# A two-direction scan by head pairs: scores and turned factors from one product each, with an identity stored beside keys and queries

## The reference

```
def step(s, inp):
    r_t, w_t, k_t, v_t, a_t, b_t = inp
    sa = einsum('bhvk,bhk->bhv', s, a_t)
    s = s * w_t + sa * b_t + v_t * k_t          # outer products over v and k
    return s, einsum('bhvk,bhk->bhv', s, r_t)
```

## Time and profile before

| | us |
|---|---|
| three runs | 4171.22 (median), 4166.51, 4188.89 |
| the profiled execution, its own time | 4177.35 |
| its span in the profile | 4175.7 |
| busy in the span: PE / PEld | 3887.3 (93%) / 2497.7 (60%) |
| busy: DVE / ACT / POOL | 1563.2 / 852.1 / 772.0 |
| mean granted clock of TensorE | 0.986 of full speed |

### The profile page before, as it was taken

How to read it: one execution, slowest core, us unless ns; L and a number is a source line. 1 busy time by engine, 2 the same in 40 slices (tenths; PEclk the granted TensorE clock), 3 DMA queues, 4 the chain that set the end, 5 groups by cost and what they waited for, 6 DMA issues and landing times.

```text
span 4175.7 us, 93934 instructions
## 1 busy us (share of the span) xinstructions
PE 3887.3 (93%) x40168; PEld 2497.7 (60%) x40168; DVE 1563.2 (37%) x3295; ACT 852.1 (20%) x1872; POOL 772.0 (18%) x634
## 2 busy tenths in 40 slices
PE   5999999989988888888999999999999999999998
PEld 4544444455467767777444434457688854658887
DVE  1411111154644444444222212444344424525363
ACT  2200000020145545445100001115000011420000
POOL 3100000000133333333000000000334310013343
PEclk8999999999999999999999999999999999999999
DMA  8289999942200000000379996110122221102221
GB/s 347 116 321 355 361 353 358 372 183 74 84 8 16 13 12 12 12 12 13 141 333 428 429 428 280 61 61 1 69 93 81 83 87 41 41 21 81 97 85 41
DMA packets 56386, 627.10 MB, mean 150 GB/s; under 512 B 5904, under 2 KB 9232, under 8 KB 20496
## 3 DMA queue, kind: packets, MB, share of 16 engines
q1 hardware_dynamic: 49664, 599.41, 36.2%
q0 software_dynamic: 3968, 14.16, 1.2%
q10 hardware_dynamic: 2448, 9.05, 0.6%
HBM read 604.50 MB, written 18.09 MB: 149 GB/s over the span
## 4 chain that ended last, share of the span: by engine, by line
PE 83%; issue 5%; DVE 5%; DMA 4%; ACT 1%; DVEq 1%; PEld 0%; SPq 0%; ACTq 0%; PEldq 0%
PE bank L919 63%; PE bank L1401 13%; DMA ring<-slabs 2%; DMA work<-slabs 2%; PE bank L1808 1%; PE bank L947 1%; PE bank L1816 1%; PE bank L1825 1%; PE bank L1452 1%; DVE hx L2539 0%; PE bank L1814 0%; DVE work L2848 0%; PE bank L1811 0%; DVE resc L2760 0%; DVE work L2717 0%
## 5 line engine op out<-in xcount | busy, mean ns | idle before, releaser
L919 PE MATMUL bank<-ring,work 128*32 128x256 f32 (+3 forms) x7002 | 763.2, 438 | 67.4 <-DMA ring<-slabs 58.8
L919 PE MATMUL bank<-work 128*128 128x256 f32 (+7 forms) x3478 | 713.3, 416 | 13.4 <-DVE work L3233 4.8
L919 PEld LDWEIGHTS bank<-work 128*128 128x128 f32 (+3 forms) x3478 | 463.3, 178 | 247.3 <-issue 185.5
L919 PEld LDWEIGHTS bank<-ring,work 128*32 128x32 f32 (+2 forms) x7002 | 316.7, 124 | 488.6 <-issue 382.5
L919 PE MATMUL bank<-hx,ring 128*128 128x512 f32 (+1 forms) x1344 | 484.3, 514 | 4.9 <-DVE hx L2539 2.8
L919 PE MATMUL bank<-work,ring 128*128 128x256 f32 (+1 forms) x1616 | 478.6, 454 | 9.2 <-DVE work L2804 5.5
L919 PEld LDWEIGHTS bank<-work,ring 128*128 128x128 f32 x1616 | 305.3, 190 | 176.1 <-issue 130.8
L1401 PE MATMUL bank<-work 64*64 64x64 f32 x11520 | 327.1, 227 | 67.9 <-issue 54.1
L919 PEld LDWEIGHTS bank<-hx,ring 128*128 128x128 f32 x1344 | 253.5, 190 | 223.6 <-issue 201.6
L3431 POOL TENSOR_TENSOR work<-ring 128x512 f32<-128x512 f32 (+1 forms) x44 | 69.3, 1575 | 1622.1 <-ACT work L2037 1224.4
L1401 PEld LDWEIGHTS bank<-work 64*64 64x64 f32 x11520 | 293.7, 139 | 94.9 <-issue 92.4
(11 more groups left out here) (336 smaller groups left out, 4830.4 us busy)
## 6 DMA issues: line engine op xcount, KB each, us to landing
ring<-slabs SPq DMA_DIRECT2D x228, 2048.0 KB, 9.7
work<-slabs SPq DMA_DIRECT2D x48, 2048.0 KB, 18.3
work<-kv SPq DMA_DIRECT2D x18, 384.0 KB, 3.1
kv<-work SPq DMA_DIRECT2D x2, 3072.0 KB, 15.7
kv<-work ACTq DMA_DIRECT2D x6, 512.0 KB, 18.1
work<-tabs ACTq DMA_DIRECT2D x1, 2176.0 KB, 8.3
resx<-xT SPq DMA_DIRECT2D x1, 2048.0 KB, 11.2
kv<-work POOLq DMA_DIRECT2D x1, 2048.0 KB, 7.1
```

Source lines behind the costliest of these rows:

```text
L919: return pe.matmul(out, lhsT, rhs, start=(k == 0), stop=(k == n - 1))
```

## The change

- Scores and two of the three transposes come from one product. An identity is stored between the factors of each two chunks: `ar` becomes `arc` (batch 0, for two chunks: key, identity, key) and `arx` (batches 1 and 2: key, queries, identity, key, queries). An even chunk takes key, queries, identity; an odd one identity, key, queries: 192 contiguous columns, or 128 in batch 0. `bd` against these gives its scores and its transpose, `kd` the same. The transpose of `ar`'s key stays a product of its own, now within `scores`. `turned_keys` and the steps ba and kt of TensorE are gone.
- sb now fills two banks (4 and 5) and sk two (0 and 1) for every batch, in place of one each. ACT takes all of sb: NT, QB, and two copies of 256 columns (key to BK, `ar`'s to AM). DVE takes all of sk, with a copy of 256 columns, kt, that ACT had.
- `chunk_products` takes BK and QB of a chunk in one product of 128 columns, whose moving operand is two blocks of 64 columns far apart in one tile (`BKQ`); the kv terms stand behind it.
- The order of TensorE, ACT and DVE is changed as the diff shows; wu 1 moves ahead of scores 1, and nothing stands between mean and W 0.
- `decayed_sums` is four instructions on DVE in place of one; `decayed_queries` writes with another stride; four copies write the identities once, during the mixing.

```diff
-    RK_PE += [("sb", _a, 0), ("sk", _a, 0), ("wu", _d, 0), ("ba", _a, 0), ("kt", _a, 0), ("sb", _a, 1), ("sk", _a, 1)]
-    RK_PE += [("wu", _d, 1), ("wu", _d, 2)] + ([] if _d else [("mean",)]) + [("ba", _a, 1), ("kt", _a, 1)]
+    RK_PE += [("sb", _a, 0), ("sk", _a, 0), ("wu", _d, 0), ("wu", _d, 1), ("sb", _a, 1), ("sk", _a, 1), ("wu", _d, 2)] + ([] if _d else [("mean",)])
     RK_PE += [("ar", _d, 0), ("kv", _d, 0), ("sb", _a, 2), ("sk", _a, 2), ("bc", _d, 0), ("ar", _d, 1), ("kv", _d, 1)]
-    RK_PE += [("ba", _a, 2), ("kt", _a, 2), ("bc", _d, 1), ("y", _d, 1), ("kv", _d, 2), ("ar", _d, 2), ("bc", _d, 2), ("y", _d, 2)]
+    RK_PE += [("bc", _d, 1), ("y", _d, 1), ("kv", _d, 2), ("ar", _d, 2), ("bc", _d, 2), ("y", _d, 2)]
...
-    RK_DVE += [("res",), ("bonus",)] * _d + [("mt", _a, 0)]
-    RK_DVE += [("mt", _a, 1)] + ([] if _d else [("cen",)]) + [("ar", _d, 0), ("mt", _a, 2), ("bc", _d, 0)]
+    RK_DVE += [("res",), ("bonus",)] * _d + [("mt", _a, 0), ("kt", _a, 0)]
+    RK_DVE += [("mt", _a, 1), ("kt", _a, 1)] + ([] if _d else [("cen",)]) + [("ar", _d, 0), ("mt", _a, 2), ("kt", _a, 2), ("bc", _d, 0)]
...
-    RK_ACT += [("nt", _a, 0), ("wu", _d, 0), ("ba", _a, 0), ("kt", _a, 0), ("nt", _a, 1), ("wu", _d, 1), ("wu", _d, 2)]
-    RK_ACT += [("ba", _a, 1), ("kt", _a, 1)] + ([] if _d else [("sq",)]) + [("nt", _a, 2), ("ba", _a, 2), ("kt", _a, 2)]
+    RK_ACT += [("nt", _a, 0), ("ba", _a, 0), ("wu", _d, 0), ("wu", _d, 1), ("nt", _a, 1), ("ba", _a, 1), ("wu", _d, 2)]
+    RK_ACT += ([] if _d else [("sq",)]) + [("nt", _a, 2), ("ba", _a, 2)]
...
+    elif _k == "sb":
+        RK_READ[_name] = {_b: [("act", ("nt",) + _rest), ("act", ("ba",) + _rest)] for _b in (4, 5)}
+    elif _k == "sk":
+        RK_READ[_name] = {_b: [("dve", ("kt",) + _rest)] for _b in (0, 1)}
...
-        ar = [cut(ring_b, at, NCH, 2 * CH) for at in (0, 1536)]
-        E3 = ring_b[:, 3072:3840]
-        BA = [z[:, 0:2 * NCH * 2 * CH].rearrange("p (h c n) -> p h c n", h=2, c=NCH)[:, :, :, 0:CH] for z in (hxf, ring_a)]
+            blocks = z[:, 0:o].rearrange("p (m n) -> p m n", n=CH)
+            BKQ.append([blocks[:, 2 * c:2 * NCH * 2 + c - GC + 1:2 * NCH * 2 - c - GC, :] for c in range(GC, NCH)])
+        arc = [cut(ring_b, at, GC // 2, 3, CH) for at in (0, 1664)]
+        arx = [cut(ring_b, at, NCX // 2, 5, CH) for at in (384, 2048)]
+        E3 = ring_b[:, 3328:4096]
...
-                n = 2 * CH if b else CH
-                outb, = banks(p, "sb", d, b, after=[("pool", 0, "arr", d), ("dve", 0, "ara", d)])
-                outk, = banks(p, "sk", d, b)
+                banks(p, "sb", d, b, after=[("pool", 0, "arr", d), ("dve", 0, "ara", d)])
+                banks(p, "sk", d, b)
+                outb, outk = score_banks("sb"), score_banks("sk")
                 for q, c in enumerate(chunks(b)):
-                    mb = heads2(outb[:, q * 128:q * 128 + n], bd[:, c * CH:(c + 1) * CH], ar[d][:, c, 0:n])
-                    mk = heads2(outk[:, q * 128:q * 128 + n], kd[:, c * CH:(c + 1) * CH], ar[d][:, c, 0:n], across=True)
+                    odd, at = c % 2, 256 * q - 64 * (c % 2)
+                    if b:
+                        factors = arx[d][:, c // 2 - GC // 2, 2 * odd:2 * odd + 3, :]
+                        a = arx[d][:, c // 2 - GC // 2, 3 * odd, :]
+                    else:
+                        factors, a = arc[d][:, c // 2, odd:odd + 2, :], arc[d][:, c // 2, 2 * odd, :]
+
+                    def places(out):
+
+                        if b:
+                            return out[:, at:at + 192].rearrange("p (m n) -> p m n", m=3)
+                        if odd:
+                            return out[:, at:at + 128].rearrange("p (m n) -> p m n", m=2)
+                        return out[:, at:at + 256].rearrange("p (m n) -> p m n", m=2)[:, :, 0:CH]
+
+                    heads2(places(outb), bd[:, c * CH:(c + 1) * CH], factors)
+                    turned = 512 * (q // 2) + 384 + 64 * odd
+                    mb = turn2(outb[:, turned:turned + CH], a)
+                    mk = heads2(places(outk), kd[:, c * CH:(c + 1) * CH], factors, across=True)
                 mb.then_inc(rk_pe, rk.next("sb", d, b))
                 mk.then_inc(rk_pe, rk.one("sk", d, b))
-
-            def turned_keys(p, d, b):
-
-                outb, = banks(p, "ba", d, b)
-                outk, = banks(p, "kt", d, b)
-                for q, c in enumerate(chunks(b)):
-                    turn2(outb[:, q * CH:(q + 1) * CH], bd[:, c * CH:(c + 1) * CH])
-                    mb = turn2(outb[:, 256 + q * CH:256 + (q + 1) * CH], ar[d][:, c, 0:CH])
-                    mk = turn2(outk[:, q * CH:(q + 1) * CH], kd[:, c * CH:(c + 1) * CH], across=True)
-                mb.then_inc(rk_pe, rk.next("ba", d, b))
-                mk.then_inc(rk_pe, rk.one("kt", d, b))
...
-                    m = heads2(out[:, q * 128:q * 128 + CH], WU[:, c, 0:CH], BK[d][:, c, 0:CH])
+                    if b:
+                        m = heads2(out[:, q * 128:(q + 1) * 128].rearrange("p (m n) -> p m n", m=2), WU[:, c, 0:CH], BKQ[d][c - GC])
+                    else:
+                        m = heads2(out[:, q * 128:q * 128 + CH], WU[:, c, 0:CH], BK[d][:, c, 0:CH])
                     if beside is not None:
-                        mo = other_term(others, d, beside, q, 0)
-                    if b:
-                        m = heads2(out[:, q * 128 + CH:(q + 1) * 128], WU[:, c, 0:CH], QB[d][:, c - GC, :])
-                        if beside is not None:
-                            mo = other_term(others, d, beside, q, 1)
+                        for part in range(2 if b else 1):
+                            mo = other_term(others, d, beside, q, part)
...
                     scores(p, a, 0)
                     inverse_times(p, d, 0)
-                    turned_keys(p, a, 0)
+                    inverse_times(p, d, 1)
                     scores(p, a, 1)
-                    inverse_times(p, d, 1)
                     inverse_times(p, d, 2)
                     if d == 0:
                         head_sums(p, "mean", Y, "dve", ("yf", 1))
-                    turned_keys(p, a, 1)
                     chunk_products(p, d, 0, beside=0)
                     scores(p, a, 2)
                     chunk_sums(p, d, 0)
                     chunk_products(p, d, 1, beside=1)
-                    turned_keys(p, a, 2)
...
+            def factors_turned(p, d, b):
+
+                cs_ = slice(GC * b, GC * b + GC)
+                act.wait_ge(*rk_done("pe", p, "sb", d, b))
+                act.activation(BK[d][:, cs_, 0:CH].rearrange(PAIRED, i=2), factor_copies("sb", "key"), ACT.Copy)
+                copied(p, AM[d][:, cs_, 0:CH].rearrange(PAIRED, i=2), factor_copies("sb", "a"), "ba", d, b)
...
+                keys = kn.rearrange(CHUNKED, c=NCH)
+                for out, c, last in ((arc[d][:, :, 0, :], 0, GC), (arc[d][:, :, 2, :], 1, GC), (arx[d][:, :, 0, :], GC, NCH), (arx[d][:, :, 3, :], GC + 1, NCH)):
+                    m = v.scalar_tensor_tensor(out, keys[:, c:last:2, :], -1.0, lw65[:, c:last:2, 1:65], ALU.mult, ALU.mult)
+                m.then_inc(rk_dve, rk.next("ara", d))
+
+            def identities():
+
+                for d in range(2):
+                    v.tensor_copy(arc[d][:, :, 1, :], bc(eye2.unsqueeze(1), 128, GC // 2, CH))
+                    v.tensor_copy(arx[d][:, :, 2, :], bc(eye2.unsqueeze(1), 128, NCX // 2, CH))
...
+                v.tensor_copy(BK[d][:, cs_, CH:128].rearrange(PAIRED, i=2), factor_copies("sk", "key")).then_inc(rk_dve, rk.one("kt", d, b))
```

More of the change, by code:

```diff
@@ L164 @@
         RK_READ[_name] = {}
+    elif _k == "sb":
+        RK_READ[_name] = {_b: [("act", ("nt",) + _rest), ("act", ("ba",) + _rest)] for _b in (4, 5)}
+    elif _k == "sk":
+        RK_READ[_name] = {_b: [("dve", ("kt",) + _rest)] for _b in (0, 1)}
     else:
-        _by = {"sb": ("act", ("nt",) + _rest), "sk": ("dve", ("mt",) + _rest), "mean": ("dve", ("cen",)), "gate": ("dve", ("res",))}
+        _by = {"mean": ("dve", ("cen",)), "gate": ("dve", ("res",))}
         _by.update({_q: ("dve", _name) for _q in ("x0", "ar", "bonus")}, T=("lvd", _name))
@@ L617, in build @@
         ring_a, ring_b = (flat(ring[(E0 + q) % RING]) for q in (6, 5))
-        BK, AM, QB, QK = [], [], [], []
+        BK, AM, QB, QK, BKQ = [], [], [], [], []
         for z in (hxf, ring_a):
@@ L797, in rk_bank, with score_banks, factor_copies @@
             return P[list(RK_READ[name])[0]]
+        def score_banks(name):
+            b = {"sb": 4, "sk": 0}[name]
+            return PB[:, b:b + 2, :].rearrange("p x n -> p (x n)")
+        def factor_copies(name, kind):
+            b, at = {"sb": 4, "sk": 0}[name], {"key": 128, "a": 384}[kind]
+            return PB[:, b:b + 2, at:at + 128].rearrange("p x (c n) -> p x c n", c=2)
+        PAIRED = "p (q i) n -> p q i n"
         FIRST_KEYS = P[5], P[4]
@@ L2260, in score_copy @@
             def score_copy(p, d, b):
+                p3 = score_banks("sb").rearrange(CHUNKED, c=GC)
```

(26 more changed lines are left out.)

10 lines of the change are left out of this document (5 added, 5 removed).

## The result

The changed kernel takes 4183.96 us (median of 20 runs, 4176.84 to 4195.58), the kernel before 4166.55 us (20 runs, 4159.63 to 4188.89): ratio 1.0043, 95% interval 1.0035 to 1.0052. It is 17 us slower; forecast were 37 us less. The traces therefore show about equal spans and can't be subtracted to a few us; their parts can.

The account below looks back on a forecast made before the run. TensorE was taken to run out of instructions at the ends of 256-instruction blocks in the tails. Terms: -45 - 5 + 10 + 1 + 2 = -37 us, from the median 4171.22 to 4134 us; range 4098 to 4168.

Parts of the forecast that it names:

- Other engines: DVE, ACT, POOL in the half stages: `ara`'s three further starts cost 0.3 to 0.5 us before 1.04 us idle: nothing.
- -45 - 5 + 10: Terms over 16 half stages: less stall -45 us, less streaming by merged products -5 us, new bank waits +10 us.
- C: Banks 4 and 5: ACT's copies at 0.6 us each hold back scores, kv and W; slower, 4201 us; chance 0.1.
- Stalls: TensorE out of instructions in the tails: 0.7 us left, 2.8 off in each of 16, -45 us (0 to -66).
- rival A: Instruction supply bounds everything outside the level loop; a block less saves 16 x 4.1 = 66 us, 4105; chance 0.2.
- If tails fall below 14.5, A: Sign in the profile after: tails below 14.5 us would mean the supply bounds everything outside the level loop.
- rival B: Tail stalls depend on where dense blocks lie, so fewer instructions give nothing: -5 - 15 + 13, about 4164 us; chance 0.2.
- New waits: TensorE's bank waits in the half stages, for centring and ACT's copies: 7 + 5 us, counted as +10 (0 to +25).
- The centring: W of batch 0 waits for bank 6 until DVE has centred the mean: 0.85 us in 8 half stages, +7.
- The 5 us for the copies of scores and turned factors: Waits for ACT's four copies from banks 4 and 5, before scores and kv of batch 2: together +5 us.
- the term of +2: Stretch before the loop: each score group waits for all copies of the one before, about 2 x 1.2 us: +2.
- Identities and prologue: Identities written once in the mixing, +1 us, and score groups waiting for copies before the loop, +2 us.

Follow-up runs that it names:

- experiment 2: The changed kernel with one wait more, POOL starting its two products only after the four `ara` instructions of DVE: 4131.22 us, ratio 0.9912 to the kernel before.
- experiment 4: Kernel before with POOL waiting for `ara`: with `ara` in four instructions 4174.18 us, with the wait alone 4169.78 us (ratio 1.0013 each).
- Experiment 5: W's merged product alone in the kernel before: 4153.09 us; W again in two products in the changed kernel with POOL's wait for `ara`: 4147.65 us.
- experiment 6: Kernel before, same instructions, but 27 of 36 turning products of a tail stream 128 columns in place of 64: 4170.94 us, ratio 1.0007.
- experiment 7: Changed kernel with POOL's wait for `ara` and the mean in bank 3: 4124.04 us; also `ara` in two products: 4123.69; `ara` on POOL, no wait: 4125.26.

## Why the prediction was wrong, point by point

**The step that failed** is under "Other engines": "DVE's factor is four instructions in place of one of 0.96 us; three further starts cost 0.3 to 0.5 us, and DVE idles 1.04 us behind it: nothing." The cost of three further starts was not their issue but what they met: 4.5 us more on DVE (5.46 against 0.96) in a slot with 1.04 us of slack, and some 3 us of wait for PE. With that removed (experiment 2) the change gives 4131 us; 4134 were forecast, and the sign too is right. That match is in part luck: the tails, waits in them included, are 3.5 to 4.0 us shorter, 56 to 63 us in all, where 40 were forecast (-45 - 5 + 10), and the level loops, for which nothing was forecast, are longer by 14 to 21 us. No rival held this mechanism: C put the loss in ACT's copies, and the waits for ACT at L1418 are 1.4 us for L2208 and 1.2 for L2307, where before had 3.6 and 0.7. The rows that would have told stood in the trace of before and were not asked for: POOL's L3382, a 1.81 us product, with a median of 2.58, the 0.77 us that it stood behind DVE's one `ara`; and five of the 16 `ara`, of 2085 to 2457 ns, that had come second. I had read the factor in one half stage, where it came first.

**Stalls: -45 us, mis-sized.** 3.4 us of idle time a tail became 0.1, where I left 0.7 in: about 3.3 off, not 2.8, and the whole tail is 3.6 to 4.1 us shorter, near rival A's size. "If tails fall below 14.5, A" was too sharp a sign: A also wanted that nothing be given back, and in experiment 2 the level loop keeps 0.9 to 1.3 us of it (14.9 against 13.9, or 13.6 in experiment 4). 0.6 to 0.8 of that is more idle time for instructions in the loop, such as these two of experiment 2, some 2 and 7 us after the loop's start (PE's timeline):

```profile
1373.40 2.72 PE L1418 MATMUL bank<-work 64*64 64x64 f32 x105 [1.20 <-issue]
...
1378.12 0.45 PE L1418 MATMUL bank<-work 64*64 64x64 f32 x14 [1.17 <-issue]
```

The supply limits the loop's start too, which the forecast didn't see. Whether these pieces follow from where the code's blocks fall was not tried by itself. Experiment 5 hints at it: with 64 instructions more in each tail, the loops are 1.3 and 1.5 us shorter.

**The rule of the Trainium skill that I weighed** (Runtime: NRT & Kernel Launch, section Instruction fetch mechanics: crossing a block is mostly hidden): experiments 5 and 6 decide against it for this kernel, at 15 to 16 ns an instruction removed or added, and 23 us of work taken up for nothing. So rival B falls as well. Its sum was also wrong as written: -5 - 15 + 13 holds 15 us of gain that its words don't have. Without them it gives 4179 us, not 4164, and the range would have ended near there.

**New waits: +10 us, right in the sum only.** The centring cost 8.3 us by the waits and 7 by experiment 7, for 7 forecast. The 5 us for the copies of scores and turned factors did not come: no such wait stands in the 16 half stages. The waits that there are, 1.4 us for ACT's L2208 and 2.8 for DVE's L2925, lie between 1156 and 1166 us, before the loop over pairs, and belong to the term of +2 below (before had 1.1 and 0.7 us there). In their place came one that was not forecast: 4.2 us for L2864, at the start of direction 1's half stages, against 0.4 before. That the sum fits is luck.

**Identities and prologue: +3 us.** The four copies of the identity take 0.2 to 0.3 us each on DVE. From DVE's last mixture to its first copy of the stage the kernel needs 18.06 us (1149.23 to 1167.29) against 15.69 (1150.89 to 1166.58): +2.4. The 2.5 us of waits for copies just named lie in it. Right.

**What is left in the balance of the changed kernel.** The level loop is 4.1 us longer: 2.7 us of wait for L2870 (48.2 - 5.1 us, over 16), 0.6 of "issue", and 0.8 that my tally of idle pieces doesn't hold. The clock can account for it: in the loop shown PE's granted clock is 0.83, between its levels of 1.2 and 2.4 GHz, where before it was 1.00, and 448 products keep PE busy for 13.5 us in place of 10.4. PE's 3.17 us of idle time stand in that loop, but in experiment 2 a loop with no such wait also has 0.89 (15.6 us long). Over all 16 loops the mean is 0.94 before, 0.89 after and 0.92 in experiment 2. How much of the clock is due to the wait stays open.

## What to carry to other kernels

Splitting one elementwise instruction into several is not free where another engine works beside it: ask, for each start, which operands lie in SBUF and what GpSimd does then, and compare the minimum of the same line's durations with its median. An order between the two engines, even as a further wait on the one with slack, can be worth more than their overlap. And where a dense stretch of small products has idle pieces that no one released, count instructions, not columns: each one less gave 15 ns here, and more columns cost nothing that could be told from none.

## What was not expected of the hardware

- Two engines that worked on different data lengthened each other's instructions: `ara` of 0.28 to 0.42 us took up to 2.02 beside POOL, and POOL's product of 1.81 us took 2.58 behind one `ara`. Level copies with one operand in PSUM were untouched (0.425 us).
- The time doesn't show as a wait: in these rows it lies inside the duration of the instruction, so that DVE looks busier than it is: 460.7 us in the stage, against 420.8 in experiment 2 with the same instructions (1157 to 1960 us there), and 397.5 before, without the copies that it took over from ACT (21 us).
- 27 products a tail with twice the columns added 23 us to PE's busy time and, within the error, nothing to the kernel's.
